# VectorE's share of a weighted sum of gathered rows: moved from the end of the weights' step to the head of a later one

## The reference, cut to what matters

```python
def peer_ffn(h, w_q, subkeys, u_tab, v_tab):
    ...
    experts = (i1 * PEER_N_KEYS + i2).reshape(n_blk, PEER_TOKEN_BLOCK, PEER_HEADS * PEER_TOPK)
    gates = jax.nn.softmax(best_s, axis=-1)...
    def expert_block(args):
        xt, e, g = args
        act = jax.nn.gelu(jnp.einsum('td,tkd->tk', xt, jnp.take(u_tab, e, axis=0)), approximate=False) * g
        return jnp.einsum('tk,tkd->td', act, jnp.take(v_tab, e, axis=0))
```

## Time and profile before

| | |
|---|---|
| median of 3 runs | 3575.6 us (3564.45 to 3580.89) |
| profiled execution | 3569.56 us, span 3567.7 us |
| PE busy | 2629.8 us, 74% of the span |
| VectorE busy | 2088.4 us, 59% |
| GpSimd busy | 1710.3 us, 48% |
| ScalarE busy | 677.3 us, 19% |
| mean granted clock of TensorE | 0.857 of full speed |
| DMA | 1070.99 MB, mean 300 GB/s |

### The profile page before, as it was taken

One profiled execution on the slowest core, in us unless ns is written; L12 is line 12 of the kernel. 1 busy time (PEld: TensorE's weight loads), 2 busy tenths in 40 slices (PEclk: granted clock), 3 DMA queues, 4 the chain that ended last, 5 costly groups with the idle time before them and its releaser, 6 DMA issues. The chain is left out here.

```text
span 3567.7 us, 29649 instructions
## 1 busy us (share of the span) xinstructions
PE 2629.8 (74%) x8956; PEld 1513.1 (42%) x8956; DVE 2088.4 (59%) x5138; ACT 677.3 (19%) x1797; POOL 1710.3 (48%) x1540
## 2 busy tenths in 40 slices
PE   6889974568778878568688786655877878676666
PEld 1467753222345544224355563522344545232222
DVE  2453336964675564963455645599555656965555
ACT  0022200111023211111133411111133311111111
POOL 0000001645565654663354433257574766777776
PEclk9789987779889999789889897877988989788888
DMA  5432324879999999897677675679998999999998
GB/s 201 177 124 89 112 106 159 325 272 394 394 411 357 356 380 389 311 323 280 226 272 267 236 290 218 253 274 365 349 416 354 385 418 418 347 348 381 362 366 301
DMA packets 262812, 1070.99 MB, mean 300 GB/s; under 512 B 29824, under 2 KB 30592, under 8 KB 233728
## 3 DMA queue, kind: packets, MB, share of 16 engines
q0 software_dynamic: 221184, 805.40, 59.8%
q1 hardware_dynamic: 38304, 253.14, 18.3%
q10 hardware_dynamic: 3168, 10.55, 0.7%
HBM read 1065.67 MB, written 3.31 MB: 300 GB/s over the span
## 5 line engine op out<-in xcount | busy, mean ns | idle before, releaser
L631 PE MATMUL psum<-ring,wdiag 128*128 128x512 f32 x1732 | 947.6, 694 | 459.1 <-ACT wdiag L925 445.8
L1589 POOL DMA_INDIRECT ring<-in_peer_u,experts x418 | 470.2, 1125 | 1087.5 <-DVE experts L1386 630.8
L1589 POOL DMA_INDIRECT ring<-in_peer_v,experts x583 | 642.5, 1102 | 491.0 <-PE psum L631 323.7
L631 PEld LDWEIGHTS psum<-ring,wdiag 128*128 128x128 f32 x1732 | 366.7, 222 | 943.9 <-issue 907.1
L1589 POOL DMA_INDIRECT work<-in_peer_u,experts x350 | 395.8, 1131 | 162.9 <-issue 98.4
L1164 DVE SCALAR_TENSOR_TENSOR acc<-ring,wts,acc 128x1024 f32<-128x1024 f32 x144 | 185.0, 1285 | 407.8 <-issue 364.4
L719 PE MATMUL psum<-work,wring 128*128 128x128 f32 (+1 forms) x2048 | 367.5, 339 | 43.5 <-DMA wring<-in_wpack 35.3
L719 PEld LDWEIGHTS psum<-work,wring 128*128 128x128 f32 x2048 | 328.5, 201 | 98.0 <-issue 59.3
L631 PE MATMUL psum<-work,wdiag 128*128 128x512 f32 x500 | 275.7, 695 | 84.8 <-ACT wdiag L925 81.8
L1140 DVE CUSTOM_DVE_ANT_0 work<-work 128x1024 f32<-128x1024 f32 x280 | 333.7, 1221 | 6.7 <-DMA work<-in_peer_u,experts 3.8
L707 PE MATMUL psum<-wring,work 128*128 128x512 f32 (+1 forms) x672 | 301.3, 609 | 21.1 <-DMA wring<-in_wpack 14.7
(11 more groups left out here) (181 smaller groups left out, 2638.4 us busy)
## 6 DMA issues: line engine op xcount, KB each, us to landing
wring<-in_wpack SPq DMA_DIRECT2D x220, 1024.0 KB, 7.8
wring<-in_wpack SPq DMA_DIRECT2D x24, 512.0 KB, 7.4
ring<-in_peer_v,experts POOLq DMA_INDIRECT x583, 6.4
ring<-in_peer_u,experts POOLq DMA_INDIRECT x418, 6.4
work<-in_peer_u,experts POOLq DMA_INDIRECT x350, 6.5
work<-in_rows ACTq DMA_DIRECT2D x4, 1024.0 KB, 10.5
wring<-in_wpack SPq DMA_DIRECT2D x4, 896.0 KB, 10.0
work<-in_peer_v,experts POOLq DMA_INDIRECT x185, 6.5
```

Of the source, the lines that this page charges most:

```text
L631: last = nc.tensor.matmul(psum[:, 6 + q, :], wdiag[:, SUM_NO[e] % SMALL, :], row(V_SLOT[e])[:, 512 * q:512 * (q + 1)], start=(e % KSEL == ...
L1589: pool.indirect_dma_start(row(slot), None, a[table], index).then_inc(got[slot], 16)
```

## The change

In VectorE's expert step the adds of a pair stand at the head of the step that is LAG_SUM = 4 after the pair's dots, ahead of that step's own dots, and not at the end of the step two after the dots. A wait is added ahead of the weights, so that a ring place of wts isn't overwritten while an add still needs it. The bound 8 in by_vector is written as 2 * LAG_SUM, which is 8.

```diff
 def by_vector(e):
     k, every = e % KSEL, SHARE[e // KSEL]
-    return k >= 8 and k % every == every - 1
+    return k >= 2 * LAG_SUM and k % every == every - 1
...
                 def expert_step(g):
+                    p = g - LAG_SUM
+                    if 0 <= p < ALL_STEPS:
+                        for e in range(PAIR * p, PAIR * (p + 1)):
+                            if by_vector(e):
+                                add_row(e)
                     if g < ALL_STEPS:
                         l, t = EXPERT_TILES[g // STEPS]
...
                             dve.wait_ge(diags_made, sums_before(e - SMALL + PAIR, False))
+                        if e >= SMALL and sums_before(e - SMALL + PAIR, True):
+                            dve.wait_ge(rows_acc, sums_before(e - SMALL + PAIR, True))
                         nc.vector.tensor_tensor(wts[:, s:s + PAIR], acts[:, s:s + PAIR], gates[:, tk:tk + PAIR], ALU.mult).then_inc(wts_ready, 1)
-                        for e in range(PAIR * p, PAIR * (p + 1)):
-                            if by_vector(e):
-                                add_row(e)
```

## The result

Median of four runs each: 3420.01 us (3416.21 to 3423.84) against 3570.02 us (3563.19 to 3580.89) before; a fourth run, of 3563.19 us, has joined the three whose median stood at 3575.6. The ratio is 0.9577, with a 95% interval of 0.9545 to 0.9609: 150 us less, where 80 were forecast. The time lies 8 us under the low end of the range. The profiled execution took 3423.39 us, its span is 3421.6 us.

A forecast was written before the change was run, and what follows sets the result against it. No engine fills the span; VectorE's adds wait for V rows, holding up trunk work and PE. Third tile 66, fourth and fifth 12, second 2, turns -3, clock 3: 80 us off 3569.6 gives 3490 us, range 3428 to 3560.

The forecast's parts named there:

- Last tile 0, since an add that waits costs the asks nothing: Last tile: GpSimd's row of asks is the bound, so 0 us gained and length within 15 us.
- bounds of -48 and +118: Last tile: limits in us for the change in ask stretching by VectorE instructions; 0 was taken.
- the third tile's terms: Third tile: PE's idle time is the most that can be won, taken stage by stage, 66 us in all.
- fourth and fifth tile: Good part full of transfers; 6 us taken of a 10.41 us wait and 6 for the rest, 12 us.
- turns: Where tiles begin, asks and PE's closing sums may wait longer for adds: 3 us charged for five, bound 25 us.
- the wait of 32.4 us for the diagonals: Third tile, 1740 to 1892: one PE wait behind the norms, left out of the 56.5 us idle; 24 taken.
- The clock's term: Attention stretches where PE waited: PE's clock, granted at 0.78 and 0.92 of full speed, was to give 3 us more.
- Rival 1: The next dots wait for their U rows, so a wait yields 1.24 us: 3545 us; 20 in 100.
- Rival 2: Move opens a ring of V asks, PE sums, trunk work; third tile's PE idle falls 120 us: 3438 us; 18 in 100.
- Rival 3: Lone VectorE instructions stretch asks at the shared port; last tile grows 118 us: 3608 us; 6 in 100.
- The added wait: Ahead of each weights instruction, met when reached: 0 us taken, 27 us if uncovered.
- the V slots: V slots come free two steps later, but the V ask loses nothing, except perhaps one step where a tile begins.

The follow-up runs named there:

- Experiment 4: Kernel before with each add at the head of step p+3, moved past the trunk work alone: 3482.8 us, ratio 0.9772.
- Experiment 5: Kernel before with GpSimd asking V(e) behind U(e+4) instead of U(e+6), adds not moved: 3458.7 us, ratio 0.9716.
- Experiment 3: Changed kernel with adds at the end of step p+3, behind its weights and ahead of the trunk work that follows: 3414.95 us, ratio 0.958.
- Experiment 2: Kernel before with the adds moved in the last tile alone: 3540.45 us, ratio 0.9921.
- experiment 7: Changed kernel with small VectorE copies of 0.15 us ahead of each last-tile dot: one copy 3423.4 us, two copies 3448.52 us.
- experiment 1: Kernel before with the adds moved in the third tile alone: 3492.17 us, ratio 0.9791.

## Why the prediction was right or wrong

**Right: the wait and what stood behind it.** The adds' idle time in the third tile fell from 216 to 18 us (named: under 50), that of the dots rose to 36 (under 40), and the tile lost 88 us (50 to 90). Experiment 4 shows that the trunk work held up by the add was the larger part: 69 of 88. Experiment 5 shows from the other side that the V row was what was waited for. Experiment 3 adds that the trunk work behind step p+3, which the change moves the add past as well, gives nothing more.

**The step that failed: "Last tile 0, since an add that waits costs the asks nothing".** The first part held: the wait went from the adds to the dots. But the tile lost 32 us, twice the 15 that I had named. I had written the right mechanism down (an ask waits for the end of the VectorE instruction that it meets, 48 us of stretching in the kernel before), set bounds of -48 and +118 to it, and took 0 by four lone dots in the earlier trace rows. The mean ask fell to 0.996 us, where 1.12 had been named, and the stretching to 262 x (0.996 - 0.94) = 15 us. Lone dots don't start at random against the asks: most come to lie just behind an ask's start. The four lone dots could have told it. The first two began 0.36 and 0.65 us ahead of an ask and held it up; the other two, whose rows are below, began 0.14 and 0.18 us behind one and cost next to nothing.

```profile
3218.87 0.94 POOL L1589 DMA_INDIRECT work<-in_peer_u,experts  x1 [0.30 <-issue]
3219.01 1.23 DVE L1140 CUSTOM_DVE_ANT_0 work<-work,h2a 128x1024 f32<-128x1024 f32 x1 [1.18 <-DMA work<-in_peer_u,experts]
```

Experiment 2 shows the gain and experiment 7 the loss. The Trainium skill's rule (SBUF — State Buffer, section "SBUF: two separate sides") was weighed as speaking against the change. The trace agrees again that an ask is held (1.74 us for 0.94), but more separate instructions brought fewer long holds: 17 asks above 1.2 us in the last tile for 54. The rule gives the pair to whichever starts first, for its whole instruction. That part isn't borne out: 119 dots began during an ask and lasted 1.22 to 1.26 us, as the dots of the kernel before did there (1.21 to 1.26).

**Mis-sized: the third tile's terms.** By stretch, aligned on the same PE instructions:

| stretch of before | taken | measured |
|---|---|---|
| 1740 to 1892, the norms before it at 0 | 24 | 41 (1650 to 1892) |
| 1950 to 2125 | 16 | 18 |
| 2157 to 2210 | 14 | 15 |
| 2210 to 2260 | 0 | 0 |
| 2260 to 2327 | 12 | 6 |
| the rest | 0 | 8 |
| fourth and fifth tile | 12 | 13 |
| second | 2 | 9 |
| last | 0 | 32 |
| turns | -3 | inside the rows above |

At the turns PE's closing sums do wait longer for the adds, 9.7 us in all where the kernel before has 2.1 us in this row, where 3 us had been charged; how much of that the kernel's time pays, no run here shows:

```profile
PE psum L642 <- DVE acc L1168: 9.7, 4, 5.3
```

The first line of the table carries the error. I had counted the wait of 32.4 us for the diagonals as not to be won. It is 18.3 us in the changed kernel (PE's waits, 1742 to 1836):

```profile
PE psum L631 <- ACT wdiag L925: 18.3, 1, 18.3
```

The wait was fed by an add. In the kernel before (VectorE, then ScalarE; line 1439 is the first of the work that ends in the norms):

```profile
1745.98 1.28 DVE L1164 SCALAR_TENSOR_TENSOR acc<-ring,wts,acc 128x1024 f32<-128x1024 f32 x1 [8.44 <-issue]
1747.18 2.76 DVE L1439 TENSOR_TENSOR work<-work,consts 128x256 f32<-128x256 f32 x8
1755.63 0.30 ACT L907 ACTIVATE stat<-stat,consts 128x6 f32<-128x6 f32 x1 [20.10 <-DVEq L1114]
1770.54 0.39 ACT L925 ACTIVATE wdiag<-consts,wts 128x128 f32<-128x128 f32 x1
```

The weights were there at 1737.39. But in ScalarE's order the diagonal stands behind the norms' roots, and the norms began on VectorE only after the add, which had waited 8.44 us for its row. In the changed kernel the norms begin with the weights, and take the same 23 us to the diagonal. So some 10 of the 14 us are the add's wait and its own time. The other 27 us of the line lie behind 1771: 21 of idle time and 6 of PE's busy time, where I had taken 24. Within the fourth and fifth tile 14 us were won at 2700 to 2775, and 9 us given back at 2775 to 3002, in part in stretches full of transfers.

**The clock's term was too small.** I took 3 us. In the third tile alone PE's busy time fell by 14 us for the same instructions, at a granted clock of 0.91 of full speed for 0.87 and with 74 us less of pauses. In experiments 1 and 4, whose third tiles have fewer pauses too, the clock stands at 0.92 and 0.91. This is inside the table, not on top of it.

**The rivals.** Rival 1 (the wait only changes its name) happened where it was allowed to: in the second, fourth, fifth and last tile. Rival 2 (a ring) gave 120 us of idle in the third tile; 74 were measured, my own terms said 66. GpSimd's waits for PE there fell from 91 to 75 us, and those for dots from 277 to 199 us. A ring may have had a part in that; no run here tells how large. That its total of 3438 is nearer to the time is owed to the last tile. Rival 3 named the right place with the wrong sign. The added wait cost nothing that can be found, and the V slots next to nothing, as said: the one wait of GpSimd for an add is 2.9 us.

**Still open.** The third and last tile alone give 76 + 27 = 103 us, and the profiled executions put some 22 us more into the second, fourth and fifth tile and 4 into what comes before. That leaves some 20 us of the 150 that no run here assigns, part of them perhaps the 11 us by which experiment 1's other tiles came out longer.

## What to carry to other kernels

In an engine that works in order, put the instruction whose data land last behind the work that others wait for; the gain is what PE idled behind it, stage by stage, and a wait in a stretch full of transfers only changes its name. A wait that looks as if it had no choice may be fed by the same cause, so don't take it off the sum before following what made it late. Where the row of asks is the bound, look at the mean length of an ask and at how much of a VectorE instruction is left as the next ask begins, not at VectorE's idle time.

## What the runs showed of the hardware that was not expected

In the last tile an indirect ask of GpSimd takes 0.94 us and starts every 1.24 us. A VectorE instruction of two float32 inputs, 1.22 to 1.28 us long, that was under way as the ask began held it up to 1.98 us: the ask ended 0.81 us after the instruction did, in 119 of the 131 asks of the two kernels that met over 0.15 us of one. The other 12 took 0.93 or 0.94 us; they began within 0.07 us behind the start of an add. A wide instruction that began during an ask didn't stretch it (0.94 us), nor did one with 0.13 us or less to run. In the changed kernel most dots came to lie so by themselves, and stayed there when one copy of 0.15 us was put ahead of each; two copies pushed them out, for 25 us. The profile names a wait ahead of an add "issue" where it was a landing row: the 364.4 us of it went when the adds moved behind the landing, and to 15.7.
